# Gain rows of the add-and-norm places through DRAM instead of identity products

## The reference, cut to what matters

```
mod_ctx = silu(c_ctx) @ ada_w[l] + ada_b[l]      # 6 x 1024; mod_lat likewise from c
shift1, scale1, gate1, shift2, scale2, gate2 = split(mod, 6)
...
x = x + gate1 * rmsnorm(merged @ w_out, norms[1])
h2 = rmsnorm(x, norms[2]) * (1 + scale2) + shift2
f = moe_swiglu(h2, ...) if is_moe else swiglu(h2, ...)
x = x + gate2 * rmsnorm(f, norms[3])
```

## Time and profile before

| | |
|---|---|
| median of 3 timed runs | 1925.7 us (1922.33, 1925.7, 1929.22) |
| profiled execution, device time | 1921.34 us |
| profiled execution, span | 1919.5 us |
| mean granted TensorE clock | 0.971 of full speed |
| busy, share of the span | PE 93%, DVE 52%, ACT 41%, POOL 13% |
| DMA | 350.74 MB, 183 GB/s on the mean |

### The profile page before, as it was taken

One profiled execution on the slowest core, in us unless ns is written; L12 is line 12 of the kernel. 1 busy time (PEld: TensorE's weight loads), 2 busy tenths in 40 slices (PEclk: granted clock), 3 DMA queues, 4 the chain that ended last, 5 costly groups with the idle time before them and its releaser, 6 DMA issues.

```text
span 1919.5 us, 32369 instructions
## 1 busy us (share of the span) xinstructions
PE 1785.3 (93%) x14036; PEld 1503.8 (78%) x14036; DVE 1002.3 (52%) x1290; ACT 787.2 (41%) x1094; POOL 257.6 (13%) x221
## 2 busy tenths in 40 slices
PE   5999899999989999998998999999988799899994
PEld 3888688887869999877997788888867356468884
DVE  2866345444745443337963445546448044257885
ACT  3345622234344222224365422325345143347774
POOL 2610033231000000005300223320002000000001
PEclk9999899999999999998999999999999999899997
DMA  9652052216552344337521412226458978959994
GB/s 350 221 196 94 1 210 67 89 46 209 176 197 71 126 131 131 132 135 259 209 88 50 165 64 93 89 89 219 172 212 297 376 253 287 373 191 335 374 381 146
DMA packets 186387, 350.74 MB, mean 183 GB/s; under 512 B 5097, under 2 KB 60417, under 8 KB 185744
## 3 DMA queue, kind: packets, MB, share of 16 engines
q1 hardware_dynamic: 182464, 335.01, 49.5%
q0 software_dynamic: 3792, 13.80, 2.0%
HBM read 319.43 MB, written 29.36 MB: 182 GB/s over the span
## 4 chain that ended last, share of the span: by engine, by line
PE 81%; ACT 5%; DVE 5%; DMA 5%; SPq 2%; issue 2%; POOL 0%; POOLq 0%; DVEq 0%; ACTq 0%
PE bank L1100 6%; PE bank L1671 5%; PE bank L1102 5%; PE bank L1101 5%; PE bank L1640 5%; PE bank L1641 5%; PE bank L1643 5%; PE bank L1528 3%; PE bank L1526 3%; PE bank L1527 3%; PE bank L1136 3%; PE bank L1138 3%; PE bank L1137 3%; PE bank L1341 2%; PE bank L1478 2%
## 5 line engine op out<-in xcount | busy, mean ns | idle before, releaser
L1102 PE MATMUL bank<-hT_hi,ring_split 128*128 128x384 f32 x576 | 196.1, 340 | 0.0
L1777 ACT ACTIVATE ring_split<-ring 128x1024 fp32r<-128x1024 f32 (+2 forms) x84 | 119.5, 1440 | 180.1 <-DMA ring<-in_ffn_w_up 102.5
L2635 DVE TENSOR_TENSOR ring_split<-ring,ring_split 128x2048 fp32r<-128x2048 f32 (+1 forms) x28 | 73.9, 2670 | 142.7 <-ACT ring_split L1777 142.7
L1100 PE MATMUL bank<-hT_hi,ring_split 128*128 128x384 f32 x384 | 142.4, 371 | 4.3 <-DVE modv L2306 2.9
L721 DVE TENSOR_TENSOR ring_split<-ring,w_upper_a 128x1536 fp32r<-128x1536 f32 (+2 forms) x54 | 96.5, 1814 | 76.9 <-PE bank L1671 68.7
L1138 PE MATMUL bank<-ring_split,hT_hi 128*128 128x256 f32 x480 | 135.6, 283 | 0.0
L1101 PE MATMUL bank<-hT_lo,ring_split 128*128 128x384 f32 x384 | 130.9, 341 | 0.0
L1671 PE MATMUL bank<-ring,hT 128*64 128x256 f32 (+1 forms) x592 | 110.4, 513 | 17.6 <-DMA ring<-in_moe_w_up 14.0
L1528 PE MATMUL bank<-hT_hi,ring_split 128*128 128x384 f32 x352 | 118.8, 337 | 0.0
L1526 PE MATMUL bank<-hT_hi,ring_split 128*128 128x384 f32 x352 | 117.6, 334 | 0.0
L1527 PE MATMUL bank<-hT_lo,ring_split 128*128 128x384 f32 x352 | 117.2, 333 | 0.0
(11 more groups left out here) (427 smaller groups left out, 4406.1 us busy)
## 6 DMA issues: line engine op xcount, KB each, us to landing
ring<-in_w_in SPq DMA_DIRECT2D x28, 2048.0 KB, 9.0
ring<-in_ada_w SPq DMA_DIRECT2D x24, 2048.0 KB, 13.0
ring<-in_moe_w_gate SPq DMA_DIRECT2D x32, 1024.0 KB, 8.1
ring<-in_moe_w_up SPq DMA_DIRECT2D x32, 1024.0 KB, 10.3
ring<-in_moe_w_down SPq DMA_DIRECT2D x16, 1536.0 KB, 9.1
ring<-in_w_branch SPq DMA_DIRECT2D x8, 1536.0 KB, 12.4
ring<-in_ffn_w_gate SPq DMA_DIRECT2D x11, 1024.0 KB, 5.4
ring<-in_ffn_w_up SPq DMA_DIRECT2D x11, 1024.0 KB, 7.9
```

What stands on the lines that cost most here:

```text
L1100: mm(out, hi, hT_hi[:, k], start=k == 0, stop=False)
L1102: last = mm(out, lo, hT_hi[:, k], start=False, stop=k == KT - 1)
```

## The change

The sixteen calls of `gain_row` and the sixteen copies on ScalarE are gone. GpSimd stores each pair of rows from `mod` into a DRAM tensor of its own, number by number (`gains_out`: two stores of 128 partitions x 8 numbers), and loads it back with every partition reading the same row (`gains_in`). The first pair of a layer is stored behind the 16 weight subtractions and loaded behind the reload of x; the second pair of layer 0 is stored right behind that and loaded when the output product is done; the second pair of layer 1 is stored when the routed rows have left, and loaded in four quarters. VectorE waits for the loads (`gr_in`) where it waited for the copies. At the end the rows lie in four pieces of 512 in other buffers, so `y_add` multiplies in two halves.

```diff
@@ -116,7 +116,7 @@
 
 
 PER = dict(proj_mm=N_PROJ, proj_ev=N_PROJ, x_rt=6, x_dg=6, xt_p=16, h_a=8, h_d=8, h_hi=16, h_v=16,
-           y_mm=6, y_rt=6, xk=6, gr_mm=8, gr_ev=8,
+           y_mm=6, y_rt=6, xk=6, gr_st=64, gr_in=32,
            pads=1, conv=12, silu=3, dsq=1, dst=9, droot=1, qkn=9, kvt_mm=6, kvt_ev=6,
            ba_v=1, ba_l=1, g_ok=1, gc_mm=1, gc_v=1, gc_e=1, beg=1,
            a_sq=1, a_ss=1, a_rt=1, a_ok=1, tr_mm=6, tr_ev=6, v_rt=1, v_ok=1,
@@ -387,7 +387,9 @@
         side_h, side_sg, side_xs = H[:, 1216:1472], H[:, 1472:1728], H[0:SIDE, 1728:1728 + D]
         h2tok = v3(H[:, :], NT)
         yrow = h2tok, v3(ring[:, 0:NT * D], NT)
-        grow, gjunk = v3(ring[:, SLOT:SLOT + 2 * D], 2), ring[:, 2 * SLOT:2 * SLOT + D]
+        gjunk = ring[:, 2 * SLOT:2 * SLOT + D]
+        grow = (KK_[:, 0:512], KK_[:, 1024:1536]), (OT[:, 4096:4608], CV[:, 4096:4608])
+        gain_dram = nc.dram_tensor("gain_rows", (2 * DEPTH, 2, D), F32, kind="Internal").ap()
 
         def set_end(units):
 
@@ -914,6 +916,18 @@
             pool.wait_ge(s_slot[slot(0)], full(0))
             pool.dma_start(RX[:, 6144:6144 + NMASK], cst_d[:, NRES:NRES + NMASK]).then_inc(mask_in, 16)
 
+            def gains_out(layer, idx):
+
+                pool.wait_ge(mod_ok, 4 * layer + 2 * idx + 2)
+                for g in range(2):
+                    dst = gain_dram[2 * layer + idx, g].rearrange("(k p) -> p k", p=P)
+                    pool.dma_start(dst, mod[:, layer, 2 + 3 * idx, :, g], allow_slow_non_contiguous=True).then_inc(S["gr_st"], 16)
+
+            def gains_in(layer, idx):
+
+                wait(pool, "gr_st", layer, 32 * (idx + 1))
+                pool.dma_start(gain_rows[idx], gain_dram[2 * layer + idx].partition_broadcast(P)).then_inc(S["gr_in"], 16)
+
             for layer in range(DEPTH):
 
                 wait(pool, "xk", layer, 0)
@@ -946,6 +960,7 @@
                 for q in range(4, 16):
                     lower_block(q // 4, q % 4)
 
+                gains_out(layer, 0)
                 wait(pool, "a_ok", layer, 1)
                 pool.dma_start(new_k[0, layer].rearrange("t h d -> t (h d)"), qkv[:, 0, 512:768]).then_inc(kv_out, 16)
                 pool.dma_start(new_v[0, layer].rearrange("t h d -> t (h d)"), qkv[:, 0, 768:1024]).then_inc(kv_out, 16)
@@ -994,6 +1009,11 @@
                 wait(pool, "oc_mm", layer, 3)
                 wait(pool, "br_mm", layer, 24)
                 pool.dma_start(xt, xpark.rearrange("p (t n) -> p t n", t=NT)).then_inc(unparked, 16)
+                gains_in(layer, 0)
+                if layer == 0:
+                    gains_out(0, 1)
+                    wait(pool, "y_mm", 0, NT)
+                    gains_in(0, 1)
 
             wait(pool, "br_ev", 1, 8)
             pool.dma_start(route, cst_d[:, NRES + NMASK:NCST]).then_inc(route_in, 16)
@@ -1011,6 +1031,13 @@
             n_items = pool.value_load(table[0:1, NI:NI + 1], min_val=N_FIX, max_val=MAX_ITEMS)
             for done in moved:
                 pool.wait_ge(done, 32)
+            gains_out(DEPTH - 1, 1)
+            wait(pool, "gr_st", DEPTH - 1, 64)
+            wait(pool, "y_mm", DEPTH - 1, NT)
+            for g in range(2):
+                for half in range(2):
+                    src = gain_dram[2 * DEPTH - 1, g, 512 * half:512 * (half + 1)]
+                    pool.dma_start(grow[g][half], src.partition_broadcast(P)).then_inc(S["gr_in"], 16)
             for s in range(N_SIDE):
                 pool.wait_ge(side_yt, FG + 2 * s + 2)
                 r0 = SIDE0 + SIDE * s
@@ -1082,13 +1109,6 @@
                             wait(pe, "x_dg", layer, NT * idx + t + 1)
                         last = mm(B[T_BANK[k % 4]][:, t * P:(t + 1) * P], xt[:, t, k * P:(k + 1) * P], diag[:, t], start=True, stop=True)
                     last.then_inc(S["xt_p"], 1)
-
-            def gain_row(layer, a, g, half, b):
-
-                for k in range(4):
-                    last = mm(B[b][:, k * P:(k + 1) * P], mod[:, layer, a, 4 * half + k, g:g + 1].to_broadcast([P, P]), ident,
-                              start=True, stop=True)
-                last.then_inc(S["gr_mm"], 1)
 
             def bank_free(layer, n):
 
@@ -1483,10 +1503,6 @@
                                 last = mm(out, low[:, q, cs], o_hi[:, q], start=False, stop=k == 3)
                         last.then_inc(S["br_mm"], 1)
                 ada_quads(at["wo"], 0)
-                pe.wait_ge(mod_ok, 4 * layer + 2)
-                wait(pe, "br_ev", layer, 7)
-                for half in range(2):
-                    gain_row(layer, 2, 0, half, 2 + half)
                 ada_turn(at["wo"], 0, ada_buf)
                 wait(pe, "o_lo", layer, O_LO.index("me7") + 1)
                 for t in range(NT):
@@ -1508,11 +1524,6 @@
                             last.then_inc(S["y_mm"], 1)
                         elif t == NT - 1:
                             last.then_inc(S["wo_mm"], 1)
-                    if t == 0:
-                        for half in range(2):
-                            wait(pe, "gr_ev", layer, half + 1)
-                            gain_row(layer, 2, 1, half, 2 + half)
-                wait(pe, "gr_ev", layer, 4)
                 wait(pe, "xk", layer, 2)
                 ada_quads(at["nb"], 7)
                 turn_x(layer, 1)
@@ -1550,16 +1561,12 @@
 
                 if layer == 0:
                     gate_up(0)
-                    pe.wait_ge(mod_ok, 4)
                     pe.wait_ge(ada_cp, set_end(at["nb"]))
-                    for q in range(4):
-                        gain_row(layer, 5, q // 2, q % 2, ROW_BANK[q])
                     with pe.Fori(0, 2) as it:
                         for j in range(1, 1 + FF_LOOP):
                             gate_up(j, it)
                     for j in range(1 + 2 * FF_LOOP, FF_GU):
                         gate_up(j)
-                    wait(pe, "gr_ev", layer, 8)
                     for u in range(FF_DN):
                         j, ks = FF_GU + u, ff_rows(u)
                         pe.wait_ge(w_lo, ff_part(j, None, 0))
@@ -1764,10 +1771,6 @@
                     wait(pe, "xk", layer, NT + 2)
                     ada_quads(at["n4"], 7)
 
-            pe.wait_ge(mod_ok, 4 * DEPTH)
-            for q, b in enumerate((0, 1, 6, 7)):
-                gain_row(DEPTH - 1, 5, q // 2, q % 2, b)
-
         @block.scalar
         def _(act):
             go = nc.scalar.activation
@@ -1790,12 +1793,6 @@
                     wait(act, "xk", layer, t + 1 if idx else t + 1 - NT)
                 link(go(junk, xt[:, t], ACT.Square, accum_out=xss[:, t:t + 1]))
                 go(xss[:, t:t + 1], xss[:, t:t + 1], ACT.Sqrt, bias=eps1, scale=1.0 / D).then_inc(S["x_rt"], 1)
-
-            def row_copies(layer, idx, qs, bank):
-
-                for q in qs:
-                    wait(act, "gr_mm", layer, 4 * idx + q + 1)
-                    copy(gain_rows[idx][:, q // 2, 512 * (q % 2):512 * (q % 2 + 1)], B[bank[q]][:, :]).then_inc(S["gr_ev"], 1)
 
             def h_upper(layer, idx, split=True, between=None):
 
@@ -2069,7 +2066,6 @@
                 split_out("w18b")
                 split_out("w19a")
                 split_out("w19b")
-                row_copies(layer, 0, range(4), (2, 3, 2, 3))
                 y_root(layer, 0, 0)
                 x_root(layer, 1, 0)
                 y_root(layer, 0, 1)
@@ -2097,7 +2093,6 @@
                     h_upper(layer, 1)
                     ff_upper(0, None, slice(1, 2))
                     unit(0)
-                    row_copies(layer, 1, range(4), ROW_BANK)
                     with act.Fori(0, 2) as it:
                         for j in range(1, 1 + FF_LOOP):
                             unit(j, it)
@@ -2252,9 +2247,6 @@
                     item_upper(last_item, True)
                     break
             link(go(vss, vss, ACT.Sqrt, bias=eps1, scale=0.0))
-            for q, b in enumerate((0, 1, 6, 7)):
-                wait(act, "gr_mm", DEPTH - 1, 4 + q + 1)
-                copy(grow[:, q // 2, 512 * (q % 2):512 * (q % 2 + 1)], B[b][:, :]).then_inc(S["gr_ev"], 1)
 
             def scaled(t):
                 act.wait_ge(moved[t], 64)
@@ -2635,7 +2627,7 @@
                         v.tensor_tensor(lo, raw, hi.bitcast(F32), ALU.subtract).then_inc(w_lo, 1)
 
                 dve.wait_ge(unparked, 16 * (layer + 1))
-                wait(dve, "gr_ev", layer, 4)
+                wait(dve, "gr_in", layer, 16)
                 for t in range(NT):
                     add_step(layer, 0, t)
                     if t == NT - 1:
@@ -2673,7 +2665,7 @@
                         unit(j)
                     for u in range(1, FF_DN):
                         lower_parts(FF_GU + u)
-                    wait(dve, "gr_ev", layer, 8)
+                    wait(dve, "gr_in", layer, 32)
                     add_step(layer, 1, 0)
                     add_step(layer, 1, 1)
                     x_diag(1, 0, 0)
@@ -2871,9 +2863,12 @@
 
             def y_add(t):
```

(7 more changed lines are left out.)

## The result

| | before | changed |
|---|---|---|
| median, us | 1926.61 (1922.33 to 1930.29, 6 runs) | 1936.09 (1930.45 to 1938.49, 6 runs) |
| profiled execution, device time | 1921.34 us | 1937.08 us |
| profiled execution, span | 1919.5 us | 1935.3 us |
| mean granted TensorE clock | 0.971 | 0.960 |

The ratio is 1.0043, 95% interval 1.0024 to 1.0061: slower, against a forecast of 1923.8 and a range up to 1931.0.

A forecast was written before the change was run, and what follows sets the result against it. TensorE was taken to bound the kernel, DMA costing only where its engines are full. Gains of 7.7 us against costs of 0.4, 0.2, 4.8 and 0.4 gave -1.9 us: 1923.8 from a median of 1925.7, range 1918.0 to 1931.0.

The forecast's parts named there:

- (c): Last place: single-number stores hold the DMA engines many times longer than 64-byte runs; at 12.8 us, 1934.5; chance 0.12.
- the term for the last pair's stores: Layer 1 behind the experts, DMA engines full: two single-number stores cost 2.1 us, ends 1.1 and 12.8.
- Products in the feed-forward: Layer 0 feed-forward: 32 product records gone, the loop moves up by the whole 3.49 us.
- Layer 1: Removed products gain 0.8 us ahead of the output product and 1.70 us after the first tile.
- Layer 0 after the first tile: Removing 16 product records there gains 1.70 us, since the stage's end hangs on TensorE's progress.
- (d): Layer 0 ahead of the modulation's turn: longer TensorE idling shifts its clock, about 1.7 us either way; no separate chance.
- First load: Layer 0, behind the reload of x: delays output weights, cost 0.4 us, ends 0 and 1.2; layer 1, 0.
- Feed-forward weights: Layer 0, second pair's load starting behind the third output tile: cost 0.2 us, ends 0 and 0.6.
- Last loads: Layer 1 expert stage, DMA engines full: the last pair's loads cost 2.7 us.
- The sign to watch: Expert stage: TensorE's waits for expert weights in the full stretch rise by some 5 us from 7.3.
- (b): Expert stage hides its transfers, leaving 6.7 us of gain: 1919.0 us; chance 0.2.
- End: VectorE scales each output tile in two halves, two of three tiles in the last chain: cost 0.4 us.

The follow-up runs named there:

- shifted code: Kernel with the last pair by identity products and the other three through DRAM, plus 160 idle waits heading TensorE's list: 1919.57 us, ratio 0.9962.
- The filler's kernel: Kernel with last pair by identity products and TensorE's code shifted, plus eight removed products put back unread in layer 0's idle gap: 1924.62 us, ratio 0.9989.

## Why the prediction was wrong

The mechanism that decided was one of the rivals, (c), to which I gave 0.12; the step of my own sum that failed is the term for the last pair's stores, "I take 1.07 per store, 2.1 for a pair". It measured 8.5 to 9.6 us (moved), 9 us (doubled), and 7.6 us of full rate by the trace. A gather in 1024 runs of 64 bytes was no neighbour of a store in 1024 runs of 4 bytes; by the run with the same bytes in 128 runs, the pair costs little. My upper end for the pair, 12.8, held, and the place where it turns slower by over 0.3%, 9.8 us, was about right. The range of the whole did not reach the end that I kept for this term. With 9 in place of 2.1 my sum would have given 1930.7, just inside the range. Of the 5.4 us that the changed kernel lies above that, some 2 are the second step that failed, layer 0 (below), and 0.9 the median of the kernel before, which rose; the rest is no more than the uncertainty.

Point by point:

- *Products in the feed-forward*, 3.49 us: 188.0 (mean of the two profiles) to 184.30, 3.7 us. Right.
- *Layer 1*, 0.8 and 1.70: 5.17 to 4.48 and 62.21 to 60.40, 0.69 and 1.81 us. Right.
- *Layer 0 after the first tile*, 1.70: "so the 1.7 us arrive". It did not. The stretch went from 62.6 to 63.4 us in the changed kernel, and to 64.4 to 65.5 in others with the same edits there. 1.2 us of it is the later landing of the feed-forward weights behind a code fetch, which no term of mine had and which TensorE's wait for the third diagonal shows. The rest goes with longer spells at half clock, my (d), priced there at 1.7 us; that they are its cause isn't shown, and why they are longer stays open, since neither moving the transfers nor filling the gap shortened the stretch.
- *First load*, 0.4: the split of the output weights came 2.4 us late, near my upper case of 2.7, where I had TensorE 1.2 us late. It had no wait there, and the run in which that load waited (64.95 us) was no faster: it costs nothing that shows.
- *Feed-forward weights*, 0.2: they came 1.3 us late, from the code fetch and not from the load behind the third tile.
- *Last loads*, 2.7: 1.5 to 2.7 us, each uncertain by 5. It agrees, and so would 0.
- *First pair, cost 0*: the stretches there vary by more than it could be; open.
- *The second pair's stores in layer 0* had no cost in my sum. They made a hole as deep as the last pair's (39 GB/s from 543 to 549), and it cost nothing that shows: TensorE has no wait at it, and the run that moved it away was no faster. That "in all other places nothing waits", as (c) has it, was right.
- *The sign to watch*, waits for expert weights up by some 5 us: they rose by 1.3, which I had set down as the sign of (b), while the kernel lost by (c). The sign was badly chosen, since the delay appeared in another wait and in the clock.
- *End*, 0.4: 28.9 to 30.1, and 29.5 on the mean of the ten kernels with the halves: 0.6 us.
- *No loss of GpSimd's own wait* (13.43 us): right, the first side tile was stored as planned.
- *The base.* 1923.8 came from the median less 1.9. With the sizes above, the sum of the terms is -3.7 - 2.5 + 0.8 (layer 0 as a whole) + 9 + 2.1 + 0.6 = +6.3 us; the ratio gives +8.3, interval 4.6 to 11.8.
- *The rule on writes under 512 bytes* of the Trainium skill ("DMA: Bandwidth & Descriptors", Specifications) gave an estimate of 4.3 us for the pair. Its sum, +0.2, had the sign right by a margin that nothing could have measured; the trace shows nearly twice the 4.3. The advice of the same page, Rules for kernel authors, to make a strided last dimension contiguous, is what the 64-byte run bears out: those runs are under 512 bytes too, and cost nothing that shows.

The best version of the study keeps the last pair on TensorE, where it costs nothing, and takes the three others through DRAM: 0.9976 (0.9957 to 0.9996), with shifted code 0.9962 (0.9941 to 0.9983), against 1.0043 for the change as made. The filler's kernel, of the same design, had 0.9989, so the gain is some 0.1 to 0.4%, and the interval of the last one includes none.

## What to carry to other kernels

Look at how finely a store is cut, not at its bytes: turn a column into rows on chip, or store it in the order in which it lies, when weights are in flight on the same engines. Taking work off the busiest engine is worth its length only where that engine is waited for; work at an idle end costs nothing and should stay. Before a stage is compared between kernels, profile one kernel twice, and leave out the stretches that differ. And when a shape has no row of its own, as the store of single numbers had none here, let the range of the whole reach the upper end of that term.

## What the runs showed of the hardware

- Two stores of 1024 single numbers each, 8 KB in all, cost 7.6 us of the transfer rate of all 16 engines, and land in 12.8 us each (median of eight); 128 runs of 64 bytes cost nothing that shows. The packets of the stores themselves are recorded as 256 bytes and mostly 80 ns; the time shows in the weight packets beside them, up to 5.3 us in the last place, 7.4 in layer 0 of the same kernel and 7.3 in the feed-forward, where packets of the same size otherwise take 0.08 and 0.05 us.
- A load that every partition reads from the same row cost no more than its bytes: packets of 8192 bytes at 0.32 us (median), beside 0.16 us for 4096 bytes.
- A code fetch of 16 KB is one packet on one DMA engine, mostly 0.9 to 1.5 us. Where one fell among the packets of a weight that was waited for, that weight was ready 1.1 to 1.3 us later than with the fetch moved. Taking the identity products out of TensorE's list moved the fetches, and so did 80 instructions at its head.
- The granted clock of TensorE falls from 1.0 to 0.5 (2.4 to 1.2 GHz) in spells; in layer 0 of the kernel before one of 3.4 us lies in the earlier trace rows, behind an idle time of 2.73 us. Two profiles of the same kernel had 112.7 and 143.8 us of them.
